# Differential attention heads: the score matmuls of a job's two maps issued as one group, alternating between the two row groups of TensorE

## What is computed

```python
def diff_attend(q, ks, vs, lam):
    scale = q.shape[-1] ** -0.5
    def blk(qb):                                  # 128 query tokens at a time
        s = concatenate([einsum('bqhid,bkhid->bhiqk', qb, kk) for kk in ks], axis=-1) * scale
        p = softmax(s, axis=-1)                   # i = 0, 1: the two maps of a head
        pd = p[:, :, 0] - lam * p[:, :, 1]
        ...                                       # out = pd @ v over latent and cached keys
```

## Time and profile before

| what | us |
|---|---|
| median of 3 runs | 5171.96 |
| lowest and highest of them | 5168.32, 5173.55 |
| the profiled execution's own time | 5164.73 |
| its span in the trace | 5162.9 |

### The profile page before, as it was taken

The page is one execution under the profiler, slowest core; times in us unless marked ns, Lnnn a source line. Parts: engine busy times, 40 slices in busy tenths (PEclk is TensorE's granted clock), DMA queues, the critical chain, the costliest instruction groups (busy, mean ns, idle before and its releaser), DMA issues.

```text
span 5162.9 us, 46892 instructions
## 1 busy us (share of the span) xinstructions
PE 4427.5 (86%) x14388; PEld 2284.0 (44%) x14388; DVE 3387.4 (66%) x7266; ACT 1951.4 (38%) x5074; POOL 1663.2 (32%) x1600
## 2 busy tenths in 40 slices
PE   7889878998899888888888887999888987777777
PEld 4674355434645333344544434644464632222222
DVE  4249754777787677775444885777778767676544
ACT  1210443443233434565533034534323343333333
POOL 3003021323243453443332322132224344344332
PEclk8899989999999999999999998999999999999999
DMA  7752416999799999999999133189979999999998
GB/s 286 267 176 74 173 65 239 347 351 362 286 420 420 415 420 420 412 394 417 406 419 412 57 130 130 62 324 349 354 279 420 415 416 422 421 421 419 422 421 351
DMA packets 277115, 1677.27 MB, mean 325 GB/s; under 512 B 31808, under 2 KB 31856, under 8 KB 112384
## 3 DMA queue, kind: packets, MB, share of 16 engines
q0 software_dynamic: 190896, 1365.43, 65.5%
q1 hardware_dynamic: 82944, 302.03, 15.9%
q10 hardware_dynamic: 3024, 6.82, 0.3%
HBM read 1667.33 MB, written 6.82 MB: 324 GB/s over the span
## 4 chain that ended last, share of the span: by engine, by line
DMA 42%; PE 29%; DVE 17%; ACT 6%; issue 6%; POOL 0%; SPq 0%; DVEq 0%; ACTq 0%; POOLq 0%
DMA arena<-experts,bsb 26%; DMA arena<-experts,peidx 13%; PE ps L2217 13%; PE ps L1804 5%; DVE arena L1495 4%; DVE arena L1707 3%; DVE arena L1406 2%; PE ps L1912 2%; DMA wring<-w 2%; PE ps L2069 2%; PE ps L2091 2%; PE ps L1780 1%; ACT T L1069 1%; ACT L1065 1%; ACT bsb L1066 1%
## 5 line engine op out<-in xcount | busy, mean ns | idle before, releaser
L2217 PE MATMUL ps<-arena,T 128*128 128x512 f32 x4096 | 1970.8, 615 | 442.4 <-ACT T L1069 436.5
L1707 DVE CUSTOM_DVE_ANT_0 arena<-arena,h_sb 128x1024 f32<-128x1024 f32 x1024 | 1250.4, 1225 | 868.8 <-DMA arena<-experts,bsb 857.5
L680 POOL DMA_INDIRECT arena<-experts,bsb x1024 | 1093.0, 1067 | 1745.6 <-PE ps L2217 1590.0
L2217 PEld LDWEIGHTS ps<-arena,T 128*128 128x128 f32 x4096 | 727.3, 192 | 1568.8 <-ACT T L1069 934.6
L1065 ACT ACTIVATE bsb<-T 128x1 f32<-128x1 f32 x1024 | 206.0, 201 | 1312.6 <-DVE T L1707 1309.6
L1804 PE MATMUL ps<-h_sb,wring 128*128 128x256 f32 (+2 forms) x2304 | 517.4, 381 | 35.5 <-DVE h_sb L1446 13.7
L2128 PE MATMUL ps<-h_sb,wring 128*128 128x512 f32 x1024 | 457.4, 600 | 33.7 <-DVE arena L1632 31.5
L1804 PEld LDWEIGHTS ps<-h_sb,wring 128*128 128x128 f32 x2304 | 379.9, 196 | 184.6 <-issue 152.6
L663 POOL DMA_INDIRECT arena<-experts,peidx x224 | 251.5, 1123 | 617.3 <-DVE arena L1406 581.5
L1396 DVE CUSTOM_DVE_ANT_0 arena<-arena,h_sb 128x1024 f32<-128x1024 f32 x256 | 312.6, 1222 | 186.8 <-DMA arena<-experts,peidx 185.5
L1069 ACT ACTIVATE T<-ident,bsb 128x128 f32<-128x128 f32 x1024 | 410.9, 401 | 33.5
(11 more groups left out here) (326 smaller groups left out, 4539.1 us busy)
## 6 DMA issues: line engine op xcount, KB each, us to landing
wring<-w SPq DMA_DIRECT2D x576, 512.0 KB
arena<-experts,bsb POOLq DMA_INDIRECT x1024
bsb<-bias POOLq DMA_DIRECT2D x16, 512.0 KB, 3.8
arena<-subk POOLq DMA_DIRECT2D x4, 1024.0 KB, 10.6
arena<-experts,peidx POOLq DMA_INDIRECT x256, 8.1
arena<-v_scratch POOLq DMA_DIRECT2D x64, 64.0 KB, 2.0
x_sb<-xT POOLq DMA_DIRECT2D x1, 2048.0 KB, 14.3
v_scratch<-arena ACTq DMA_DIRECT2D x8, 256.0 KB, 2.0
```

The lines of the kernel that those rows point to most:

```text
L680: gp.indirect_dma_start(rows[:, n % NS, :], None, experts, bass.IndirectOffsetOnAxis(ap=eidx[:, t % 2, i:i + 1], axis=0)).then_inc(row_in[ ...
L1707: v.tensor_tensor_reduce(e, e, htok(t), 1.0, 0.0, ALU.mult, ALU.add, dots[:, t % 2, i:i + 1]).then_inc(dot, 1)
L2217: mm = pe.matmul(ps[:, 6 + half, :], diag[:, n % ND, :], rows[:, n % NS, D + half * 512:D + (half + 1) * 512], start=(i == 0), stop=(i == ...
```

## The change

For the differential jobs the two calls of `map_scores` become one call of `pair_scores`. It issues the four program matmuls of a job in the order: 512 latent keys of map 0, 512 latent keys of map 1, 128 cached keys of map 0, 128 cached keys of map 1. The banks are the same as before. One wait now stands ahead of all four, `exp_done >= NMAPS * l + m` with the even m: the exponentials of both maps of the job before are done. Each map still raises `s_ready` at its last matmul. The local jobs keep `map_scores`. The streams of DVE, ACT, POOL and SP are the same instructions in the same order.

```diff
+                def pair_scores(m):
+                    n = MAP_JOB[m][0]
+                    kind, h, t = JOBS[n]
+                    if m >= 2:
+                        pe.wait_ge(exp_done, NMAPS * l + m)
+                    maps = [keys(kind, h, i, t) for i in range(2)]
+                    for part, (at_col, width) in enumerate(((0, LAT), (LAT, PAST))):
+                        for i, (q, ks) in enumerate(maps):
+                            mm = pe.matmul(ps[:, 2 * i + part, 0:width], q, ks[part][0], start=True, stop=True, skip_group_check=True)
+                            if part:
+                                mm.then_inc(s_ready, 1)
...
                 for n, (kind, h, t) in enumerate(JOBS):
                     for m in maps_at(n, 2):
-                        map_scores(m)
+                        if JOBS[MAP_JOB[m][0]][0] == "nat":
+                            map_scores(m)
+                        elif MAP_JOB[m][1] == 0:
+                            pair_scores(m)
```

## The result

The changed kernel takes 5219.17 us, the median of four runs (5212.18 to 5230.1); the kernel before, with one more run beside it, 5172.76 us (5168.32 to 5182.8). The ratio is 1.0094 with a 95% interval of 1.0073 to 1.0116: slower by 38 to 60 us, 46 by the medians. The prediction was 5250 in a range of 5212 to 5276. The direction, the place and the mechanism came out as written. The size did not: +46 us where +78 was forecast, near the low end of the range, and in the interval of 5210 to 5235 that had been given a chance of 0.24, not in that of 5235 to 5264 with 0.62. It is the size of the first rival, the clock that stays up, though the clock did not stay up.

What follows compares the result with a forecast made beforehand. PE's own work was taken to bound the differential jobs by 0.2 us, DVE's chain right behind. Layer 0 +35.4, layer 1 +39.1, front +1.8, stage end +2 gave +78.3: 5250 us, range 5212 to 5276.

Steps and rivals of the forecast that it cites:

- the first rival: Differential jobs: clock stays up except in each layer's first three jobs; about +50 us, 5222; 5210 to 5235 given 0.24.
- The bound and the wait: Differential jobs: pair waits for map 2n+1's exponential, closing a loop through ACT, PE, DVE; 6.54 us for 4.93, full clock.
- The overlap of a pair: Scores on PE: two maps cost what one costs, 1.38 us at full clock, 2.51 at half; alternating buys no more.
- the rival without overlap: Alternating pairs don't overlap on PE: 9 to 9.5 us a job, +110 to +125 us, 5282 to 5297; chance 0.08.
- The clock: PE in the differential jobs: half clock about three quarters of the time, 7.85 us a job, ends 6.54 and 8.25.
- POOL's share: First differential jobs of a layer: POOL's work beside them slows DVE; 3 us added a layer.
- The ends of the stage: Job 1's scores start 0.92 us later, twice +1.8; step after job 14 and first local jobs +1 a layer, +2.
- The sum: Layer 0 +35.4, layer 1 +39.1, front +1.8, stage end +2: together +78.3 us, 5250 on the median.
- The rule on idle time: PE's clock falls only after long idle; none in the new job exceeds 1.73 us, so it stays up: first rival's time.

Runs made afterwards that it cites:

- the run with the wait alone: Kernel before, old matmul order, but a job's first map also waits for both exponentials of the job before; 5222.55 us, ratio 1.0097.
- the run with the short piece first: Changed kernel, but map one's 512 columns keep the old wait and its 128-column piece precedes the second map; 5207.76 us, ratio 1.009.
- the exponential first: Changed kernel with ACT's exponential of map 2n+3 ahead of the copies for job n in the differential jobs; 5207.88 us, ratio 1.0066.
- the values done twice: Differential jobs' value matmuls issued twice: on the changed kernel 5216.18 us; on that kernel with ACT's exponential moved ahead of its copies 5199.59 us, ratio 1.0067.
- the exponential first without the merged wait: Kernel before, no pairs, with ACT's exponential of map 2n+3 ahead of the copies for job n; 5163.01 us, ratio 0.9979.

## Why the prediction was right, and where its size was off

**The bound and the wait.** Right, and shown by the run with the wait alone. The loop at the full clock was forecast at 6.54 us and measured 6.60; of the difference 0.06 is in its first piece, 2.50 us for 2.44. The other three pieces came out to the hundredth.

**The overlap of a pair.** Right: 1.35 us for eight records, and the rival without overlap is out. That alternating adds nothing was argued from the earlier trace rows and is now shown by the run with the wait alone (1.36 us in the old order).

**The clock.** This term was mis-sized, and it makes up most of the error. The prediction took the half clock for three quarters of the time and, worse, let it lie on all pieces of the loop alike: 7.85 us a job, between 6.54 and 8.25. Measured are 97.17 / 14 = 6.94 and 98.01 / 14 = 7.00. There are two reasons. The clock was down for less of the time: PEclk 0.80 over the 14 steps of layer 0 and 0.82 in the steady part mean 40% and 36% of the time at 0.50. And it was down in the right place. In the steady part the steps are 6.91, 6.60 and 6.98 us over and over, and the pair is at the full clock in each; the half clock falls on values (2.31 us, hidden in PE's idle time) and transposes (1.07 and 1.15 for 0.76, which cost 0.3 to 0.4 us). Where it falls otherwise, as after the reordered exponential, a step costs 7.09 for 5.94. The first step of a layer, all at the half clock, took 8.15 us for a forecast of 8.25, so the price was right and the share was wrong. In numbers: with the measured share of 40% the forecast's own formula gives 0.4 * 8.25 + 0.6 * 6.54 = 7.22 us a job, 0.63 less than 7.85; where the half clock fell gives the other 0.25. Over 28 steps that is 17.5 and 7 us. What makes the chip lower the clock in this loop, and raise it again, no run here shows.

**POOL's share.** I added 3 us a layer for DVE being slowed beside POOL. It did not come: the earlier trace rows has the slow stretch at 690 to 702, but after the change L1598 takes 0.89 us at most in the whole trace. Nor do the other steps of `job_probs` in these jobs slow down (L1594 0.63 us at most, L1597 0.15). Before, POOL's bias additions (L652) ran beside them:

```profile
691.39 0.68 DVE L1597 TENSOR_TENSOR st<-st,lam 128x1 f32<-128x1 f32 x1
...
697.71 1.31 DVE L1598 SCALAR_TENSOR_TENSOR T<-T,st 128x640 f32<-128x640 f32 x1
```

These take 0.15 and 0.89 us elsewhere. After the change the additions of layer 0 run from 687.03 to 689.79 and from 693.79 to 696.55, between the L1598 of 685.32, 692.43 and 699.40, so none of them meets `job_probs`. That is a matter of where they happen to fall: in the run with the short piece first two L1594 take 1.10 us again.

**The ends of the stage.** From the first scores to L1598 of job 0 it is 677.17 - 667.38 = 9.79 us in layer 0, for 677.93 - 669.11 = 8.82 before: +0.97 for the 0.9 forecast; +1.2 in layer 1. The step after job 14 was put at +1 a layer and is 4.95 us in both layers, for 4.71 and 6.32 before, -1.1 in all: layer 1's had met the half clock before the change and not after it.

**The sum** in trace numbers: +43.9 for the 28 steps (forecast +74.5), +2.1 at the front (+1.8), -1.1 behind (+2): +45 of 47.5; the rest lies elsewhere, within what two executions differ by. Of the 30.6 us by which the steps fell short, 24.6 are the clock's and 6 POOL's. That the first rival's sum (+50) lies near is in part luck: it put 10.3 us on six early half-clock steps, which cost 5.6 over 6.60 us each, and 6 us on POOL, which cost nothing, and left out the half clock in the 22 later steps, which cost 4.8.

**The rule on idle time.** The Trainium skill (TensorE: Matmul & The Clock Gate, Why this matters for your kernels) would have kept the clock up, since no idle time of the steady part is longer than 1.74 us. Here the granted clock fell again and again with PE busy for 64% of the steady part, so the rule isn't enough by itself. The time it led to (5222) was nearer than the forecast, but not because the clock stayed up.

## What to carry to other kernels

When two waits are merged so that work can be issued together, the merged wait is the later one, and all that used to start behind the earlier one moves: before doing it, close the loop through the engines that feed that wait, here transposes, ACT's queue, PE, DVE. Overlap on an engine is worth something only if the engine stays the bound; here PE's work in a job at the full clock fell by a quarter (4.77 to 3.50 us) and the job grew by a third (4.93 to 6.60 us). Against a late signal there are two cures: moving its producer up in its own queue, or letting what doesn't need it go first on the consumer. On the changed kernel both helped the steps about alike (9.2 us with the exponential first, 7.6 with the short piece first), and neither made up for the merged wait. Only the exponential first without the merged wait beat the kernel before.

## What the runs showed of the hardware

- Matmuls in different row groups overlap fully in either program order: eight records in 1.35 us alternating, 1.36 us map by map, and 1.34 us for the four of one map.
- A matmul may start before one that stands ahead of it in the program, when that one's row group is busy (two 128-column records started at 746.17 and 746.38, the 512-column record ahead of them at 746.70), but its signal comes only after it: with the 128-column piece behind the other map's 512 columns the reader began 1.18 us after the wait, with the piece ahead 0.52 us. The Trainium skill (TensorE: Matmul & The Clock Gate, Part 3: Packing small matmuls) has matmuls start and end in program order; for the start the trace says otherwise, for the completion signal it agrees. So the piece that a reader waits for belongs first, even where the array would take it early anyhow.
- Extra PE work in idle time can shorten a stage: with the values done twice, the 28 steps fell from 186.0 to 171.3 us, as the mean granted clock of the stage rose from 0.76 to 0.94 in layer 0. The whole time did not show it, and on the changed kernel the same extra work, at 0.91 for 0.80, left the 28 steps at 195.2 us: there the half clock had fallen where it cost little, and now met the pair.
